# Sums of squares of the norms as two one-pass products instead of one float32 product

## What is computed

```
def rms_norm(x, w):
    y = xf * lax.rsqrt(jnp.mean(xf * xf, axis=-1, keepdims=True) + EPS)
    return (y * w.astype(jnp.float32)).astype(x.dtype)
...
        h = rms_norm(x, norm_mix_w[i])
        proj = jnp.einsum("bld,de->ble", h, w_in[i])
...
        h = rms_norm(x, norm_ffn_w[i])
        g = jnp.einsum("bld,df->blf", h, w_gate[i])
        u = jnp.einsum("bld,df->blf", h, w_up[i])
        x = x + jnp.einsum("blf,fd->bld", jax.nn.silu(g) * u, w_down[i])
    return rms_norm(x, final_norm_w)
```

## Time and profile before

| | |
|---|---|
| median of 3 runs | 2722.69 us (2722.46 to 2722.86) |
| profiled execution, its own time | 2721.53 us |
| its span | 2719.7 us |
| TensorE (PE) busy | 2688.3 us, 99% |
| VectorE (DVE) busy | 1512.5 us, 56% |
| ScalarE (ACT) busy | 1158.6 us, 43% |
| GpSimd (POOL) busy | 25.6 us, 1% |
| mean granted TensorE clock | 0.999 of full |

### The profile page before, as it was taken

The page is one execution under the profiler, slowest core; times in us unless marked ns, Lnnn a source line. Parts: engine busy times, 40 slices in busy tenths (PEclk is TensorE's granted clock), DMA queues, the critical chain, the costliest instruction groups (busy, mean ns, idle before and its releaser), DMA issues.

```text
span 2719.7 us, 33585 instructions
## 1 busy us (share of the span) xinstructions
PE 2688.3 (99%) x13780; PEld 2179.8 (80%) x13780; DVE 1512.5 (56%) x2109; ACT 1158.6 (43%) x1690; POOL 25.6 (1%) x45
## 2 busy tenths in 40 slices
PE   9999999999999999999999999999999999999998
PEld 7767888888767888888888888887777888888887
DVE  6685444345685444344443346688788864544433
ACT  6774322225774322233222234455588463422221
POOL 0000000000000000000000000000000000000000
PEclk9999999999999999999999999999999999999999
DMA  6202332334202332332333342222223332333222
GB/s 222 76 18 94 102 100 94 98 95 147 78 17 93 101 101 93 94 100 93 101 94 95 99 139 82 78 71 70 84 76 105 126 96 96 94 101 93 97 93 66
DMA packets 75369, 256.47 MB, mean 94 GB/s; under 512 B 9040, under 2 KB 12240, under 8 KB 74832
## 3 DMA queue, kind: packets, MB, share of 16 engines
q1 hardware_dynamic: 72704, 241.21, 28.1%
q0 software_dynamic: 2512, 13.11, 1.3%
HBM read 242.22 MB, written 8.39 MB: 92 GB/s over the span
## 4 chain that ended last, share of the span: by engine, by line
PE 92%; ACT 4%; DVE 3%; issue 0%; DMA 0%; SPq 0%; DVEq 0%; ACTq 0%
PE PS L1422 27%; PE PS L1424 27%; PE PS L1423 27%; PE PS L1381 1%; PE PS L1625 1%; PE PS L1444 1%; PE PS L1445 1%; PE PS L1446 1%; PE PS L1592 1%; PE PS L1607 1%; ACT PT L1907 1%; DVE WLO L2110 0%; ACT DE L1863 0%; PE PS L1571 0%; PE PS L1671 0%
## 5 line engine op out<-in xcount | busy, mean ns | idle before, releaser
L1422 PE MATMUL PS<-HHI,WHI 128*128 128x512 f32 x2288 | 909.3, 397 | 0.0
L1424 PE MATMUL PS<-HHI,WLO 128*128 128x512 f32 x2288 | 891.4, 390 | 0.0
L1423 PE MATMUL PS<-HLO,WHI 128*128 128x512 f32 x2288 | 890.9, 389 | 0.0
L2110 DVE TENSOR_TENSOR WLO<-WR,WHI 128x1024 fp32r<-128x1024 f32 (+2 forms) x446 | 536.0, 1204 | 509.1 <-ACT WHI L1713 506.0
L1713 ACT CAST WHI<-WR 128x1024 fp32r<-128x1024 f32 (+2 forms) x446 | 457.8, 1027 | 430.4 <-PE PS L1424 406.5
L1422 PEld LDWEIGHTS PS<-HHI,WHI 128*128 128x128 f32 x2288 | 429.5, 188 | 100.5 <-issue 12.5
L1423 PEld LDWEIGHTS PS<-HLO,WHI 128*128 128x128 f32 x2288 | 429.8, 188 | 90.6 <-issue 4.6
L1424 PEld LDWEIGHTS PS<-HHI,WLO 128*128 128x128 f32 x2288 | 429.4, 188 | 90.8
L1422 PE MATMUL PS<-FHI,WHI 128*128 128x512 f32 x682 | 265.3, 389 | 0.0
L1423 PE MATMUL PS<-FLO,WHI 128*128 128x512 f32 x682 | 265.3, 389 | 0.0
L1424 PE MATMUL PS<-FHI,WLO 128*128 128x512 f32 x682 | 265.3, 389 | 0.0
(11 more groups left out here) (341 smaller groups left out, 2586.3 us busy)
## 6 DMA issues: line engine op xcount, KB each, us to landing
WR<-in_stream SPq DMA_DIRECT2D x413, 512.0 KB, 3.5
WR<-in_stream SPq DMA_DIRECT2D x32, 384.0 KB, 3.1
xkeep<-X POOLq DMA_DIRECT2D x3, 2048.0 KB, 8.1
X<-xkeep POOLq DMA_DIRECT2D x24, 256.0 KB, 5.1
ROT<-RQ SPq DMA_DIRECT2D x40, 64.0 KB, 2.0
X<-in_xin SPq DMA_DIRECT2D x8, 256.0 KB, 6.8
out<-X SPq DMA_DIRECT2D x8, 256.0 KB, 2.2
KD<-RQ SPq DMA_DIRECT2D x8, 128.0 KB, 3.8
```

The lines of the kernel that those rows point to most:

```text
L1422: e.matmul(out, hi[:, i, :], xhi, start=first, stop=False)
L1423: e.matmul(out, hi[:, i, :], xlo, start=False, stop=False)
L1424: t = e.matmul(out, lo[:, i, :], xhi, start=False, stop=final)
L2110: e.tensor_tensor(lo, raw, hi.bitcast(F32), ALU.subtract).then_inc(S["dve_low"], 1)
```

## The change

The step "sum" no longer multiplies the float32 ACC. ScalarE makes its rounded part SQH ("shi"), VectorE the difference SQL ("slo"), and TensorE multiplies both by a matrix of ones in fp32r (ONR, copied once by ScalarE ahead of norm 0's "shi") into one accumulator. The four token matmuls of norms 0, 2 and 6 and norm 5's second product stay in float32. "sum" now waits for "slo". In the planner both steps get a duration, "sum" a shorter one, the first half of the last tile's "hsum" is put 1.6 us later, and "hsq" is said to need the logarithm's table.

```diff
-    "row": (("pe", 0.68),), "trow": (("pe", 1.36),), "sum": (("pe", 0.9),), ...
+    "row": (("pe", 0.68),), "trow": (("pe", 1.36),), "sum": (("pe", 0.47),), "shi": (("act", 0.62),), "slo": (("dve", 0.7),), ...
...
-    **dict.fromkeys("root hroot rroot dta ...".split(), LOG_EXP),
+    **dict.fromkeys("root hroot hsq rroot dta ...".split(), LOG_EXP),
...
     def mean_square(self, m):
         yield from self.until(("acc", m, DT - 1))
         count = 2 if m in (*TOKEN_NORM, 5) else 1
+        yield self.add("shi", m)
+        yield self.add("slo", m)
         if m == 5:
             yield 1.6
...
         yield from self.added(("sumx", 8))
+        if h == 0:
+            yield 1.6
         yield self.add("hsum", h)
...
             elif kind == "sum":
                 m, = a
-                q.wait_ge(s_con, 32)
-                q.wait_ge(S["dve_acc"], n["acc", m, DT - 1])
+                q.wait_ge(S["dve_acc"], n["slo", m])
...
-                e.matmul(PS[o.bank["sum", m, 0]][:, :], ONES, ACC[:, :], start=True, stop=True).then_inc(S["pe_ones"], 1)
+                e.matmul(PS[o.bank["sum", m, 0]][:, :], ONR[:, :], SQH[:, :], start=True, stop=False)
+                e.matmul(PS[o.bank["sum", m, 0]][:, :], ONR[:, :], SQL[:, :], start=False, stop=True).then_inc(S["pe_ones"], 1)
...
+            elif kind == "shi":
+                m, = a
+                if m == 0:
+                    q.wait_ge(s_con, 32)
+                    e.copy(ONR[:, :], ONES)
+                q.wait_ge(S["dve_acc"], n["acc", m, DT - 1])
+                e.copy(SQH[:, :], ACC[:, :]).then_inc(S["act_square"], 1)
...
+            elif kind == "slo":
+                m, = a
+                q.wait_ge(S["act_square"], n["shi", m])
+                e.tensor_tensor(SQL[:, :], ACC[:, :], SQH[:, :].bitcast(F32), ALU.subtract).then_inc(S["dve_acc"], 1)
```

More of the change, by code:

```diff
@@ L42 @@
     **dict.fromkeys(["sum", "hsum", "rmm", "romm", "cmm", "mean"], "ones"),
-    **dict.fromkeys(["sq", "hsq", "rsq", "rosq", "csq"], "square"),
+    **dict.fromkeys(["acc", "slo"], "acc"),
+    **dict.fromkeys(["shi", "sq", "hsq", "rsq", "rosq", "csq"], "square"),
     **dict.fromkeys(["root", "hroot", "rroot", "roroot", "croot"], "rooted"),
@@ L144 @@
 TIMES = {
[1 row of a table removed]
+    "row": (("pe", 0.68),), "trow": (("pe", 1.36),), "sum": (("pe", 0.47),), "shi": (("act", 0.62),), "slo": (("dve", 0.7),), "sumx": (("pe", 0.86),),
     "rmm": (("pe", 0.86),), "swap": (("sp", 1.8),), "kdup": (("sp", 3.0),), "xT": (("pe", 0.45),), "bT": (("pe", 0.45),), "dtT": (("pe", 0.45),),
@@ L180 @@
 FUNCTIONS = {
-    **dict.fromkeys("root hroot rroot dta ex dexp gsq exp small rln dd eb roroot ldecay llog lmult croot".split(), LOG_EXP),
+    **dict.fromkeys("root hroot hsq rroot dta ex dexp gsq exp small rln dd eb roroot ldecay llog lmult croot".split(), LOG_EXP),
     **dict.fromkeys("silu zsilu xsilu cvsilu qsilu gsilu".split(), "silu"),
@@ L1187, in build @@
     SQF, SQ, HF = two_by_two("SQF", 74)
+    SQH = sb("SQH", 74, [T], F32R)
+    SQL = sb("SQL", 76, [T], F32R)
+    ONR = sb("ONR", 71.4375, [P], F32R)
     RS = sb("RS", 82, [T])
```

## The result

The changed kernel took 2727.61 us (median of 21 runs, 2724.36 to 2730.15) against 2722.46 us of the kernel before (21 runs beside them, 2720.18 to 2724.45): ratio 1.0019, with a 95% interval of 1.0013 to 1.0026. It is 5.15 us slower. The forecast was 2724.3, with a range up to 2727.0, so the time lies 0.6 us outside; rival 2, which had 4%, gave 2728.4. The profiled execution's own span is 2726.3 us, 6.6 more than before.

A forecast was written before the change was run, and what follows sets the result against it. TensorE, busy 99% of the span at full clock, was taken to bound the kernel; -2.15 (five norms) + 2.65 (norm 6) + 1.65 (norm 0) - 0.5 (end) = +1.65 on 2722.69 gave 2724.3 us, range 2721.0 to 2727.0.

The forecast's parts named there:

- rival 2: TensorE's clock falls at both long waits, norms 0 and 6: 2728.4 us, slower by 0.21%; chance 4%.
- A rule that speaks against it: New TensorE waits of 3.1 us (norm 6) and 2.4 (norm 0) might drop its clock to 1.2 GHz; longest seen, 1.7, hadn't.
- The sum: All terms, five norms, norm 6, norm 0 and the end: -2.15 + 2.65 + 1.65 - 0.5 = +1.65 us.
- the two rivals: TensorE's clock falls at norm 6's wait only (2726.4 us, 10%) or at both long waits (2728.4 us, 4%).
- The price of a fall: Slow TensorE matmuls until full clock returns: 2.05 us per fall, from the program's first six passes (4.63 against 2.6 us).
- The product: At each sum on TensorE, two fp32r matmuls take 0.45 us instead of 0.88: 0.43 us gained.
- "slo" is in time at norms 1, 2, 3, 5 and 7: TensorE doesn't wait for VectorE's difference at these five sums, margin 1.0 us at norm 2; together 2.15 us gained.
- Norm 6: TensorE waits 3.1 us at this sum for "slo", which stands behind "low" 261 on VectorE: 2.65 us lost.
- Norm 0: Later sum delays ScalarE's string to the first "hhi"; TensorE waits some 2.4 us at the transposes: 1.65 us lost.
- The end: In the last tile, the first half's "hsum" no longer waits for "hsq": 0.5 us gained, 0.8 us of cover left.
- No waits at all: Rival: no wait at norm 0 or 6, 3.5 us gained, 2719.2 us; chance 8%.
- a wait would be absorbed: Rival: one long wait absorbed or absent, 2722.2 us without norm 0's, 2721.2 without norm 6's; chance 13%.

The follow-up runs named there:

- third experiment: The changed kernel with norm 0 left as before (float32 sum at its old place), norm 6 as changed: 2724.45 us, ratio 1.0005.
- seventh experiment: The kernel before with only the change at the end (first half's "hsum" 1.6 us later, "hsq" with the logarithm's table): 2721.72 us, ratio 0.9999.
- experiment 6: The changed kernel with norm 0's sum one "trow" later than before instead of three, norm 6's three "trow" later than changed: 2719.13 us, ratio 0.9992.
- experiment 5: The changed kernel with norm 0 left as before and norm 6's sum three "trow" later: 2719.51 us, ratio 0.9991.
- the first: The changed kernel with norm 6's sum three "trow" later, so that "slo" is done when TensorE comes: 2722.56 us, ratio 0.9998.
- second experiment: The changed kernel with 13 idle products filling TensorE's wait ahead of norm 6's sum: 2726.03 us, ratio 1.0011.
- eighth experiment: The changed kernel with norm 0 left as before and norm 6's sum only one "trow" later: 2722.37 us, ratio 1.0003.
- fourth: The changed kernel with 13 idle products in norm 6's wait and 10 ahead of the first transposes behind norm 0: 2724.52 us, ratio 1.0007.

## Why the prediction was wrong

**The step that failed** is in "A rule that speaks against it": "the matmuls behind it keep their step, so at that length the clock stays at 2.4 GHz", and with it the 4% for rival 2. The sum has no term for the clock. What happened is rival 2, both waits with the clock behind them: 1.6 us behind norm 0's and 1.8 behind norm 6's in the trace of the change, 3.4 us that the forecast put at nothing. The measured 5.15 us over before lie by that rival's 5.75 (1.65 + 4.1). The row that I leaned on the earlier trace rows is one wait of 1.7 us that in one execution did no harm. The same place in other traces here, with idle times of 1.6 to 2.9 us, had a fallen clock in eight kernels of ten (0.66 to 0.83 in the stretch from 6 to 16 us; it held in the kernel before and in the third experiment), the seventh experiment among them, which doesn't touch it. On the other side, a wait of 1.4 to 1.7 us for the tile XB in block two's mixer (near 2076 us in the kernel before, [1.37 <-DVE XB L2493]) was followed by a full clock in all ten traces (granted 1.00 from 1620 to 2710 us). So at such a length it depends on the place and the execution, and one row at which a thing didn't happen bounds nothing. For waits of 2.4 and 3.1 us there was no row, as the prediction says, and it still took the harmless outcome at 86%. With no row on either side the two rivals deserved something like half of the chance. The Trainium skill states, in "TensorE: Matmul & The Clock Gate", Part 1, that an idle TensorE goes back to 1.2 GHz. The traces of the change agree with it now, behind 2.28 and 2.98 us.

**The price of a fall** in the rivals, 2.05 us by the start's matmuls, was near: 1.6 and 1.8 in the trace of the change, 1.6 by the fill at norm 6, 1.5 by the second fill, but 3.0 in the trace of the third experiment. The row that it came from was a loose measure: those six passes took 4.63 us before, 5.35 in the change's trace and 5.49 in the third experiment's.

**The product**: 0.43 us for each sum, confirmed (0.46 for two passes in place of 0.88; +3.65 from +4.10 at norm 1). That "slo" is in time at norms 1, 2, 3, 5 and 7: confirmed, no wait for SQL but norm 6's.

**Norm 6**: 3.1 us of wait forecast, 2.98 found, net loss 2.65 forecast, 2.6 found without the slow steps. **Norm 0**: 2.4 us of wait forecast, 2.28 found; the transposes are 1.68 later than norm 0's sum makes them due, forecast 1.65. In ScalarE's timeline, against the earlier trace rows, the string is as drawn, from the logarithm to the first "hhi":

```profile
32.84 0.69 ACT L1758 ACTIVATE RS<-PS,VEC 128x512 f32<-128x512 f32 x1 [4.35 <-PE PS L1495]
34.54 1.28 ACT L1807 ACT_TABLE_LOAD   x1
35.83 2.42 ACT L1807 ACTIVATE Z<-PS,RSC 128x512 f32<-128x512 f32 x4
...
39.06 1.16 ACT L1790 CAST HHI<-SQF 128x512 fp32r<-128x512 f32 x2
```

The first "hhi" has no idle time ahead of it any more (1.15 before), and is 3.79 later on the clock, of which 2.1 are the start's.

**The end**: 0.5 forecast, 0.55 in the traces, not resolved in the timed runs. The timeline of the changed kernel, against the earlier trace rows, has no wait at the first "hsum", and 0.80 us of cover at the second half's "hadd":

```profile
2711.72 0.60 PE L1482 MATMUL PS<-SQF,CON 128*128 128x256 f32 x2
...
2713.32 3.26 DVE L2229 SCALAR_TENSOR_TENSOR X<-X,VEC,SQF 128x256 f32<-128x256 f32 x8 [3.39 <-ACT SQF L1701]
...
2717.38 0.42 DVE L2218 TENSOR_TENSOR SQF<-PS,RS 128x256 f32<-128x256 f32 x1 [0.80 <-PE PS L1474]
```

**The sum again**, with the clock's two terms: 1.65 + 1.6 + 1.8 = 5.05, measured 5.15 (3.5 to 7.1 by the interval of the ratio). So close a match is partly luck: the two profiles differ by 6.6 us, of which 2.1 are the start's, and the wait for KD takes 1.3 back, which isn't the change's either, so the traces put the change anywhere from 4.5 to 5.8.

**The other rivals.** No waits at all (2719.2) is what experiment 6 makes of the change, at 2719.13 (and experiment 5, with one sum less, at 2719.51); as a forecast for the change as it stands it was rightly low. That a wait would be absorbed: it wasn't, the offset behind norm 6, 7.6 us, is still 6.6 at the end, with norm 7's sum and the tail's gain taken off.

**What stays open.** A wait of 2.3 us at norm 0 was followed by the slow clock in the change's trace and not in those of the first and second experiments:

```profile
50.66 1.15 PE L1389 MATMUL PS<-CON,RQ 128*128 128x128 f32 x8 [2.30 <-ACT RQ L1828]
51.56 0.48 PE L1430 MATMUL PS<-HHI,WHI 128*128 128x512 f32 x1
```

(the second experiment: full step after 2.30 us). That the fill there still gave 1.5 us over the second experiment suggests that it falls in most of the timed executions, but two medians whose runs spread by 2.4 and 3.1 us carry that only roughly, and why it falls in one and not in the next no run here tells.

## What to carry to other kernels

On an engine that is busy 99% of the time, a product that is moved later waits for whatever now stands ahead of its last input: read that input's engine queue at the very place (here a chain of small preparations on VectorE and one "low"), because five places out of seven were free and the waits at the other two (3.0 and 2.3 us) cost more than all seven saved (3.0). Price a new wait of TensorE of about 2 us or more as the wait plus some 1.7 us for the matmuls at half rate behind it (3.0 in one trace here), as a likely case and not a remote one, unless several traces show waits of that length in dense work with a full granted clock well behind them. Where such a wait stayed, idle products in it gave back the second part; placing norm 6's sum three "trow" later and norm 0's two earlier gave back both.

## What the runs showed of the hardware

- An idle time of TensorE of 1.63 us between dense matmuls was followed by the fall from 2.4 to 1.2 GHz (granted clock 0.83 over 10 us, eighth experiment), and so was one of 2.28 us (change, 0.88 over 14 us); one of 2.30 us was not, twice (first and second experiment, 1.00). The two of 3.0 us both were (change 0.83, third experiment 0.84 and 0.82). One of 1.4 to 1.7 us near 2076 us was not in any of ten traces (1.00).
- The fall can come late: 2 us after the work went on in the eighth experiment, with five passes of 512 columns begun at full step in between, and the slow steps went on for 3.4 us. It can also come during the wait and last longer: 6.8 us at 1.2 GHz in the third experiment.
- The times of one kernel can lie in groups about 2 us apart, near one fall's price: of the fifth experiment's 11 runs four took 2717.8 to 2717.9 us and seven 2719.1 to 2720.4. The fall at the start, there in some profiles and not in others, would make such groups; that is argued, not shown.
- Fill products with the same operands' shape as the real ones (512 columns, fp32r) held the clock in a wait: 13 in 3.14 us (granted 1.00 behind them, second experiment), 10 in 2.46 us (fourth).
